# The last expert's first gate and first up chunk, loaded in row pieces of 96, 8, 8, 8 and 8

## The reference, cut to what matters

```python
def hier_moe(xn, router_w_group, ..., w_gate, w_up, w_down):
    ...
    def block_fn(args):
        tok, wt, e = args
        xb = x2[tok]
        hb = jax.nn.silu(xb @ w_gate[e]) * (xb @ w_up[e])
        return (hb @ w_down[e]) * wt[:, None].astype(xb.dtype)
```

## Time and profile before

| what | us |
|---|---|
| median of 3 runs | 1416.28 (1416.18 to 1417.36) |
| the profiled execution, its own time | 1416.09 |
| its span, first to last instruction | 1414.3 |
| PE busy | 1210.8 (86%) |
| DVE busy | 492.8 |
| share of DMA in the chain that ended last | 42% |

### The profile page before, as it was taken

One profiled execution on the slowest core, in us unless ns is written; L12 is line 12 of the kernel. 1 busy time (PEld: TensorE's weight loads), 2 busy tenths in 40 slices (PEclk: granted clock), 3 DMA queues, 4 the chain that ended last, 5 costly groups with the idle time before them and its releaser, 6 DMA issues.

```text
span 1414.3 us, 18072 instructions
## 1 busy us (share of the span) xinstructions
PE 1210.8 (86%) x7497; PEld 708.5 (50%) x7497; DVE 492.8 (35%) x1020; ACT 253.4 (18%) x628; POOL 18.8 (1%) x88
## 2 busy tenths in 40 slices
PE   8999999999999998768599968769687686976976
PEld 6999999776568753233245314224142241422422
DVE  5599998664866421111010310111101111011113
ACT  3001111544500231020111102002020110200212
POOL 2000000000010000000000000000000000000001
PEclk9999999999999999889899979879888898898999
DMA  9958577441644899999999999999999999999996
GB/s 300 323 181 168 151 159 239 119 90 30 180 119 184 361 422 427 427 426 428 427 429 428 426 428 428 427 428 427 429 427 427 428 427 427 428 428 427 427 427 271
DMA packets 133827, 479.35 MB, mean 339 GB/s; under 512 B 48012, under 2 KB 105840, under 8 KB 108272
## 3 DMA queue, kind: packets, MB, share of 16 engines
q1 hardware_dynamic: 127104, 477.58, 86.5%
q10 hardware_dynamic: 6640, 0.58, 0.4%
HBM read 476.05 MB, written 2.10 MB: 338 GB/s over the span
## 4 chain that ended last, share of the span: by engine, by line
PE 54%; DMA 42%; DVE 1%; ACT 1%; issue 1%; POOLq 0%; POOL 0%; SPq 0%; ACTq 0%; DVEq 0%
DMA ring<-in_expert_w_up_dram 35%; PE PS L1151 14%; PE PS L1492 10%; DMA spare<-in_expert_w_up_dram 6%; PE PS L1300 5%; PE PS L1479 4%; PE PS L1193 3%; PE PS L1277 2%; PE PS L1685 2%; PE PS L1470 1%; PE PS L974 1%; PE PS L1695 1%; PE PS L1143 1%; PE PS L1212 1%; PE PS L1556 1%; PE PS L1252 1%
## 5 line engine op out<-in xcount | busy, mean ns | idle before, releaser
L1492 PE MATMUL PS<-ring,XG 128*32 128x512 f32 x1296 | 231.9, 760 | 133.8 <-DMA ring<-in_expert_w_up_dram 93.9
L1492 PEld LDWEIGHTS PS<-ring,XG 128*32 128x32 f32 x1296 | 58.1, 135 | 266.4 <-issue 263.2
L3168 DVE TENSOR_TENSOR hTe<-PS,sg 128x128 f32<-128x128 f32 (+1 forms) x31 | 9.9, 320 | 340.0 <-ACT sg L2274 339.8
L2984 DVE TENSOR_TENSOR x<-PS,x 128x1024 f32<-128x1024 f32 x41 | 50.2, 1225 | 217.2 <-PE PS L1573 215.9
L1479 PE MATMUL PS<-ring,XG 128*64 128x512 f32 x192 | 91.5, 633 | 16.7 <-DMA ring<-in_expert_w_up_dram 13.9
L2261 ACT ACTIVATE Hs<-PS 128x512 f32<-128x512 f32 x30 | 17.9, 597 | 464.1 <-PE PS L1492 342.8
L1481 PE MATMUL PS<-ring,XG 128*64 128x512 f32 x192 | 91.7, 634 | 0.0
L1573 PE MATMUL PS<-Y,SW 128*128 128x512 f32 (+2 forms) x176 | 88.9, 616 | 1.5 <-ACT ro L2370 1.5
L1492 PE MATMUL PS<-spare,XG 128*32 128x512 f32 x208 | 69.6, 830 | 23.6 <-DMA ring<-in_expert_w_up_dram 23.5
L1470 PEld LDWEIGHTS PS<-sel,xn 128*128 128x128 f32 x640 | 75.3, 191 | 12.9 <-issue 12.7
L1151 PE MATMUL PS<-hT,ring 128*128 128x128 f32 x672 | 78.8, 275 | 0.0
(11 more groups left out here) (512 smaller groups left out, 1568.4 us busy)
## 6 DMA issues: line engine op xcount, KB each, us to landing
ring<-in_expert_w_up_dram SPq DMA_DIRECT2D x53, 2048.0 KB, 23.2
ring<-in_expert_w_gate_dram SPq DMA_DIRECT2D x53, 2048.0 KB, 27.2
ring<-in_expert_w_down_dram SPq DMA_DIRECT2D x51, 2048.0 KB, 26.3
ring<-in_w_in_dram SPq DMA_DIRECT2D x17, 2048.0 KB, 11.9
spare<-in_expert_w_gate_dram SPq DMA_DIRECT2D x9, 2048.0 KB, 24.1
spare<-in_expert_w_up_dram SPq DMA_DIRECT2D x8, 2048.0 KB, 22.8
spare<-in_expert_w_down_dram SPq DMA_DIRECT2D x8, 2048.0 KB, 27.2
ring<-in_w_in_dram SPq DMA_DIRECT2D x16, 512.0 KB, 7.2
```

Source lines behind the costliest of these rows:

```text
L1492: mm = pe.matmul(PS[r:r + 32, 0, :], gathered_rows(q, 4 * c + j)[:, column:column + 32], weight_rows(slots[u], 4 * (c % 2) + j), start=(c ...
L2984: dve.tensor_tensor(y, new, old, ALU.add).then_inc(sc_added, 1)
```

## The change

For g = 186 and 187 (gate and up, c = 0 and 1, of the last expert) the one DMA of 128 partitions by 16 KB is replaced by five into the same slot and from the same place: one of partitions 0 to 95, and four of 8 partitions each (96 to 103, 104 to 111, 112 to 119, 120 to 127). Each of the five counts 16 on the slot's semaphore, and `PARTS` has 5 for these two chunks, so PE waits for 80 instead of 16 more. No byte is added, none goes elsewhere, and no other engine's instructions change.

```diff
@@ -253,6 +253,9 @@
 PARTS = {CHUNKS + 1: 2, CHUNKS + 2: 2, CHUNKS + 4: 2, CHUNKS + 5: 3, 2 * CHUNKS: 2, 2 * CHUNKS + 1: 2}
+ROW_PARTS = [slice(0, 96)] + [slice(r, r + 8) for r in range(96, 128, 8)]
+IN_ROWS = [CHUNKS * (E - 1), CHUNKS * (E - 1) + 1]
+PARTS.update({g: len(ROW_PARTS) for g in IN_ROWS})
@@ -688,7 +691,8 @@
                 for dst, src in chunk_parts(e, c, SLOT_OF[g]):
-                    sp.dma_start(dst, src).then_inc(e_loaded[SLOT_OF[g]], 16)
+                    for rows in ROW_PARTS if g in IN_ROWS else [slice(0, P)]:
+                        sp.dma_start(dst[rows], src[rows]).then_inc(e_loaded[SLOT_OF[g]], 16)
```

## The result

| | before | changed |
|---|---|---|
| median, runs side by side (us) | 1416.44 | 1437.66 (1436.45 to 1437.91) |
| ratio to before | | 1.0148, 95% interval 1.0136 to 1.0160 |
| span of the profiled execution (us) | 1414.3 | 1436.2 |
| PE busy (us) | 1210.8 | 1215.3 |

A forecast was written before the change was run, and what follows sets the result against it. Expert-weight loads bound the kernel, its end hanging on g = 189's landing. Two chunks' 19.2 us extra, less a third for stagger (12.8), less the 5.2 us lead, gave +7.6 on 1416.28: 1423.9, range 1414.4 to 1428.

The forecast's parts named there:

- What bounds the kernel: DMA streams expert weights for 880 us; the end hangs on the landing of g = 189 at 1388.76.
- Fewer rows on some engines: Two cut chunks: eight engines finish 2.45 us later, the others 2.45 earlier; PE could gain at most 1.7 us.
- A: The forecast: last expert's small transfers collide in SBUF, +7.6 us, 1423.9, own range 1419 to 1428; chance 0.58.
- B: Last expert's loads: no collision, engine halves come level, -1.7 us, 1414.6 (1414.4 to 1416); chance 0.22.
- C: Last expert's loads: loaded engines are the late ones; 1418.7 without collision, +12.8 or 1429.1 with it; chance 0.12.
- D: Small transfers spread over all 16 engines or start on different ones, so nothing shifts: 1416.3; chance 0.06.
- Where the rows land: In SBUF, row groups take about 3.4 GB/s a row, whoever writes; small transfers collide, +7.6 us.
- 6 x 0.61: Each loaded engine's six rows of the 96-row transfer, at the free rate of 0.61 us a row.
- 2.7 us: Time of one 8-row transfer, taken as the middle between bounds of 0.61 and 4.8 us.
- I take off a third: 12.8: Loaded engines' 19.2 us delay cut to 12.8 for stagger of up to 3 us; the 5.2 us lead then leaves +7.6.
- PE behind the first pair: A longer wait may slow the first pair's products by 2.4 us; 1.71 of idle absorbs all but 0.7, range only.
- Issue: SP's eight more DMAs cost 1.45 us a chunk, moving the next issue to 1355.1, hidden by some 18 us of queue.

The follow-up runs named there:

- step 4: Kernel before with g = 24 and 25, some 800 us before the end, cut instead of the last expert's chunks; with the change's own cut 1435.97 us (1.0141).
- The extra transfers: Kernel before plus eight unused transfers of 8 rows by 8 KB, issued ahead of g = 186: 1417.52 us (1.0008).
- 96 + 32 rows: Changed kernel with each of the two chunks as one transfer of 96 rows and one of 32: 1433.59 us (1.0126).
- the queue program: Separate program: SP issues five 2 MB loads without waits, second and third cut, without or with engine halves set apart; all whole takes 27.21 and 34.86 us.
- 64 + 64: Changed kernel with each of the two chunks as two transfers of 64 rows: 1432.94 us (1.0115).
- turned round: 64 + 64 with the upper half first, run only in the queue program: +11.4 us alone, +12.4 with the halves apart.
- every fourth row: Changed kernel with each 8-row transfer taking every fourth row of the last 32 instead of neighbouring rows: 1437.86 us (1.0153).

## Why the prediction was right or wrong

**What bounds the kernel: right.** The loads do, and a delay of their landing came out at the end in full, at the last expert and at step 4 (19.5 us for 20.0 alone). But the end no longer hangs on g = 189, as the prediction had it, but on g = 187: by the packets g = 189 was through at 1409.4, and PE, busy with what followed the first pair, came to it only at 1410.7.

**Fewer rows on some engines: right for six of eight, and without effect.** The extra transfers went mostly to engines in front, as A and B assumed, and two of the eight engines were behind, which is C's case; that C's 1429.1 was nearer than A is chance, since it too has 12.8 for the collision. D, nothing shifted, falls with the same run, where eight engines carried them all. The lead that the prediction read from rows 5 was right: 5.2 us there, 5.4 by the packets of g = 189, with 3.1 us within the first half. But it could not be used, and nothing came of the 1.7 us of gain.

**Where the rows land: the mechanism right, the step from it to the sum wrong.** The sum was +7.6 us for the delay of the landing, and 21.5 were measured. Three terms, in the order of the working:

1. *"6 x 0.61" for the 96 rows.* This is the step that failed first. The prediction applied its limit of 3.4 GB/s a row to the 8-row transfers and let the 96-row one run freely. It does not: 96 + 32 rows take 8.8 us alone instead of 4.9, and the rate in the changed kernel is halved from 1361, before any 8-row transfer is reached (by the packets, at about 1368). By the prediction's own reading of rows 6 (64 rows, 232 GB/s), a transfer that doesn't go over all 128 rows had to be suspected.
2. *"2.7 us" for a transfer of 8 rows.* 1.95 measured, inside the bounds of 0.61 and 4.8, and 0.75 too high. For the loaded engines the two errors nearly cancel: 14.5 us a chunk forecast, 4.9 + 20.0 / 2 = 14.9 measured in the queue program. The upper term, 19.2 for both chunks, was right within 1 us of the 20.0 measured.
3. *"I take off a third: 12.8. From this their lead of 5.2 goes."* Here 11.6 of the 19.2 us were given away, and this is why the forecast was low. The lead is no cushion. The prediction let the half behind go unhampered ("it isn't the last any more"), but the whole rate is halved with all 16 engines busy (229 GB/s at a share of 1.04), and two engines on one port slow each other, the rightful one too. The proof is the uncut chunk ahead, g = 185: only the engines behind had any of it left, and it came so late that PE idled 4.72 us for it. Being apart made 64 + 64 dearer, by 4.2 us and turned round by 1.0, not cheaper. And the stagger takes little or nothing off: the change's cut costs 20.0 with the engines together and 18.1 with the halves apart (alone), and 19.5 and 21.2 in the kernel early and at its end. The prediction would have had 7.6 to 12.8.

Without term 3 the sum would have been 1416.3 + 19.2 = 1435.5. The stated upper bound of +31 was left outside the range with A's own range, which made the range too narrow: its upper end took in the discounts as if they were known.

**PE behind the first pair: right.** Forecast: the cold products (6.07 in rows 2) cost what exceeds the 1.71 us of idle, 0.7. Measured: 5.76, and 0.4 over.

**Issue: right.** 1.6 us for the next issue, 1.45 forecast, hidden; five DMAs by columns cost nothing that can be told.

**What would show it.** The rate was to be "well under 420 with the share near 1" in 1366 to 1385: 221 and 131 in the rows above, and already from 1361. The second pair's start was to be at 1396 for A and was at 1410.7. A plateau at half rate was to come again at the run-out, with the halves changed over, and did not: 330, 156 and 51 GB/s in the three rows from 1413 to 1419 are one fall, and that was B's sign. By the packets the two groups of eight are gone by then: most engines end their share of g = 189 between 1401 and 1405, single ones at 1394.8 and as late as 1409.4, where before it was 1380.3 to 1383.4 for one group and 1386.6 to 1388.3 for the other. It gained nothing, since every landing was late by then.

**Open.** Why every fourth row saves 7 us over neighbouring rows when alone, 4.4 at step 4 and nothing at the last expert (+21.5 beside +21.2). The intervals are 2.4 us to either side, so the 4.4 is hardly clear. That the distance of the engines is in it is likely by the 64 + 64 row of the table, but with small transfers the queue program didn't show it; there the engines set behind were the ones that carry them, in the kernel they are mostly in front, and that arrangement wasn't tried. A version of the last loads over all 128 rows with the engines level wasn't tried either.

## What to carry to other kernels

Cut a bandwidth-bound load by columns, not by rows: five pieces of all 128 partitions were free, two pieces of 64 rows halved the rate of 16 busy engines for longer than their own transfer. When a load gets slower by where it lands, cost the whole stretch in which it is in flight, with every transfer before and behind it, and don't deduct a lead of some engines from it. A DMA share near 1 says nothing of the rate; read the GB/s beside it. And a plateau at half rate where the loads run out says that the engines have drifted apart: look for instruction packets, which here fell on eight engines only.

## What the runs showed of the hardware

A group of four rows takes 26 to 28 GB/s, with one engine on it or four, and shares this with another group: 57 GB/s into 8 neighbouring rows, 105 into 16, 197 to 229 into 64, 428 into 128. Which engine writes a row showed no effect by itself (9.20 and 8.45 us for the two halves of the rows); what costs is two at one group at once. One 16 KB packet of the instruction queue q8 sets the DMA engine that carries it back by 1.55 us, and in 800 us thirty of them, all on the same eight engines, took these from 1.2 to 5.4 us behind the others. The price of one and the same cut grew from 11.4 to 16.6 us between step 4 and step 31 of the kernel, with nothing but the place changed. And a queue that runs at half rate holds up the issuer too, here without cost: the last issue of SP, 0.46 us before, took 13.57.
